# Modulation panels moved from plain fp32 fills to split products inside the feed-forward loops

## The reference

```python
# block 1, layer 0: attention output, one norm per head of 128
o = rms_norm(o, sub_gain) * (1.0 - lam_init);  mix = o.reshape(b, s, 1024) @ w_o
# both layers
h = h + conv_gated_ffn(rms_norm(h, ffn_norm[i]), w_in, conv_w, conv_b, w_out)   # 1024 -> 5632 -> 2816 -> 1024
h = h + (p[i] @ w_proj) * sigmoid(rms_norm(h, ple_norm[i]) @ w_gate)
# block 2, layer i: w_mod[i] is 1024 x 3072; c and c_ctx are single rows
mod_x = silu(c) @ w_mod[i] + b_mod[i];  mod_c = silu(c_ctx) @ w_mod[i] + b_mod[i]
sh, sc, g = split(mod, 3);  hx = rms_norm(x, norm_g[i]) * (1 + sc_x) + sh_x   # and x + g_x * yx at the layer's end
```

## Time and profile before

| | us |
|---|---|
| median of three runs | 1387.62 (1386.74 to 1389.39) |
| the profiled execution | 1387.44 |
| its span in the trace | 1385.7 |
| TensorE busy | 1313.0 |
| VectorE busy | 913.4 |
| ScalarE busy | 683.8 |
| GpSimd busy | 375.7 |

### The profile page before, as it was taken

How to read it: one execution, slowest core, us unless ns; L and a number is a source line. 1 busy time by engine, 2 the same in 40 slices (tenths; PEclk the granted TensorE clock), 3 DMA queues, 4 the chain that set the end, 5 groups by cost and what they waited for, 6 DMA issues and landing times.

```text
span 1385.7 us, 24959 instructions
## 1 busy us (share of the span) xinstructions
PE 1313.0 (95%) x9168; PEld 1146.1 (83%) x9168; DVE 913.4 (66%) x1397; ACT 683.8 (49%) x1207; POOL 375.7 (27%) x390
## 2 busy tenths in 40 slices
PE   6989999999999998999999999999989999999996
PEld 5877899999988886798999999878845588987656
DVE  6868667777767696656777777745257547453674
ACT  5554445555535577634555555434367613422662
...
GB/s 303 176 236 170 185 137 204 183 181 183 182 128 135 131 145 122 1 289 129 214 183 183 183 183 159 88 92 76 102 21 1 22 246 104 182 101 91 46 1 31
DMA packets 52656, 191.60 MB, mean 138 GB/s; under 512 B 6048, under 2 KB 6304, under 8 KB 52320
## 3 DMA queue, kind: packets, MB, share of 16 engines
...
q10 hardware_dynamic: 720, 0.57, 0.1%
...
## 4 chain that ended last, share of the span: by engine, by line
PE 72%; DVE 9%; issue 9%; ACT 7%; POOL 2%; DMA 1%; SPq 0%; DVEq 0%; ACTq 0%; POOLq 0%
PE G L400 12%; PE G L402 12%; PE G L401 12%; PE A L400 6%; PE A L402 6%; PE A L401 6%; PE R L525 3%; PE R L606 3%; DVE WL L1050 2%; ACT WH L1657 2%; PE A L928 1%; PE R L400 1%; PE R L402 1%; PE R L401 1%; DMA RAW<-in_wst 1%
## 5 line engine op out<-in xcount | busy, mean ns | idle before, releaser
L1050 DVE TENSOR_TENSOR WL<-RAW,WH 128x1024 fp32r<-128x1024 f32 x295 | 393.7, 1341 | 304.4 <-ACT WH L1657 303.9
L1657 ACT ACTIVATE WH<-RAW 128x1024 fp32r<-128x1024 f32 x295 | 310.5, 1057 | 433.8 <-PE G L402 310.9
L400 PE MATMUL G<-XH,WH 128*128 128x256 f32 (+1 forms) x1336 | 402.1, 301 | 11.3 <-DVE WL L1050 7.5
L401 PE MATMUL G<-XL,WH 128*128 128x256 f32 (+1 forms) x1336 | 398.2, 298 | 0.0
L402 PE MATMUL G<-XH,WL 128*128 128x256 f32 (+1 forms) x1336 | 398.0, 298 | 0.0
L400 PEld LDWEIGHTS G<-XH,WH 128*128 128x128 f32 x1336 | 256.1, 192 | 22.8 <-issue 11.5
L401 PEld LDWEIGHTS G<-XL,WH 128*128 128x128 f32 x1336 | 256.2, 192 | 7.3
L402 PEld LDWEIGHTS G<-XH,WL 128*128 128x128 f32 x1336 | 256.2, 192 | 7.1
L400 PE MATMUL A<-HH,WH 128*128 128x256 f32 x352 | 99.8, 283 | 0.0
L401 PE MATMUL A<-HL,WH 128*128 128x256 f32 x352 | 99.6, 283 | 0.0
L402 PE MATMUL A<-HH,WL 128*128 128x256 f32 x352 | 99.6, 283 | 0.0
...
## 6 DMA issues: line engine op xcount, KB each, us to landing
RAW<-in_wst SPq DMA_DIRECT2D x295, 512.0 KB, 3.6
...
```

What stands on the lines that cost most here:

```text
L400: mm(out, lh, rh, start=start, stop=False, skip_group_check=True)
L401: mm(out, lh, rl, start=False, stop=False, skip_group_check=True)
L1050: v.tensor_tensor(WL[:, slot, :], RAW[:, raw, :], WH[:, slot, :].bitcast(F32), ALU.subtract).then_inc(w_lo, 1)
L1657: act(WH[:, slot, :], RAW[:, raw, :], ACT.Copy).then_inc(w_hi, 1)
```

## The change

- 16 of the 48 modulation panels stay plain fills, all of them before and behind the attention of layer 0: 12 ahead of it, five in each of its 18 steps instead of six, then 14, 6 and 6. All other fills are gone.
- The other 32 panels are stored in another order (128 rows of two k blocks by 512 columns each) and are done as split products, 16 in each feed-forward. GpSimd's queue loads a panel into one of four slots (gathers), ACT makes its rounded copy RH at the end of a turn (high), GpSimd the rest RL after its hidden work (rest), and TensorE does four matmuls of 32 stationary columns by 512 (refill): after each of tiles 7 to 21, and the sixteenth between the last two down products. The stationary side SCR holds silu(c) rounded in two columns and its rest in two more. RH and RL are single buffers. Four panels give one row of 512 results, which ACT copies to YR (row); the fifth copy comes in ple.
- Behind pp, 16 matmuls with a selecting matrix of 4x2 turn and add the rows (turn_gathered), once a layer; DVE adds the biases later (gathered). The turns inside block 1's layer 1 and block 2 are gone.
- The head norm works on a token-major output OTOK: the value product writes tokens on the partitions, GpSimd squares each head as it comes, DVE sums per head and scales by one number per token and head, and TensorE transposes into the A banks, from which ACT and DVE make XH and XL, in two groups of four heads.
- The embeddings are split into XH and XL 8 and 9 in the feed-forward's opening, so that pp needs no HH and HL, and pp is followed at once by the gathering and pg. The squares of H for pg's norm are made by ACT (squared) and summed by GpSimd (sum_of_parts). The order of XH in layer 0's pg follows GATE.

```diff
+        SCR = sb("SCR", [P, KD, 32], F32R)
...
-        OT0 = B[:, 4096:6144].rearrange("p (n t) -> p n t", t=T)
+        OTOK = B[:, 4096:6144].rearrange("p (a c) -> p a c", a=2)
...
+        YR = B[0:32, 2048:4608]
+        RR = RM[:, 0:4, :]
+        RH = XH[:, 12:16, :].rearrange("p n t -> p (n t)")
+        RL = XL[:, 12:16, :].rearrange("p n t -> p (n t)")
...
+            def refill(layer, s, i):
+
+                if s == 0:
+                    pe.wait_ge(r_y, i + (2 + 5 * layer))
+                pe.wait_ge(r_lo, i * 4 + (5 + PLAIN * layer + s))
+                for c in range(2):
+                    for w in (RH, RL):
+                        m = mm(O[0:32, :], SCR[:, 2 * s + c, :], w[:, 512 * c:512 * c + 512],
+                               start=(s == 0 and c == 0 and w is RH), stop=(s == 3 and c == 1 and w is RL),
+                               skip_group_check=True)
+                m.then_inc(m_used, 1)
+
+            def turn_gathered(layer):
+
+                pe.wait_ge(r_y, 1 + 5 * (layer + 1))
+                for t in range(PLAIN):
+                    m = mm(O[:, 2 * t:2 * t + 2], YR[0:4, 512 + t * P:512 + (t + 1) * P], SEL, start=True, stop=True,
+                           skip_group_check=True)
+                m.then_inc(m_tr, 1)
...
-                for k in range(2):
-                    m = mm(out[:, k * P:T], V0[:, k, h * P:(h + 1) * P], pt[:, 0, k, k * P:T], start=(k == 0),
-                           stop=(k == 1), skip_group_check=True)
+                for qt in range(2):
+                    for k in range(qt + 1):
+                        m = mm(out[:, qt * P:(qt + 1) * P], pt[:, 0, k, qt * P:(qt + 1) * P], V0[:, k, h * P:(h + 1) * P],
+                               start=(k == 0), stop=(k == qt), skip_group_check=True)
...
+            def heads_turn(g):
+
+                for tt in range(2):
+                    pe.wait_ge(hn_ok, 2 * g + tt + 1)
+                    for i in range(4):
+                        m = nc.tensor.transpose(A[2 * g + tt][:, i * P:(i + 1) * P],
+                                                OTOK[:, tt, (4 * g + i) * P:(4 * g + i + 1) * P], IDT)
+                    m.then_inc(hn_tr, 1)
...
             pe.wait_ge(tm_ev, 8)
             pe.wait_ge(tm_v, 4)
+            fill(12)
             pe.wait_ge(bias_ok, 1)
-            attention("l0", scores_l0, value_l0, 6)
-            for c in range(4):
-                fill(5)
-                head_stat(HN["l0_o"] + c, ONES)
-            fill(48)
+            attention("l0", scores_l0, value_l0, 5)
+            fill(14)
+            heads_turn(0)
+            fill(6)
+            heads_turn(1)
+            fill(6)
             for u in range(4):
-                gemm_unit(U0["l0_o"] + u, START["l0_o"] + 2 * u, 0, KD, 8, 2, fresh=XS["l0_o"] if u == 0 else None)
-            turn_modulators(0, A[0])
+                gemm_unit(U0["l0_o"] + u, START["l0_o"] + 2 * u, 0, KD, 8, 2,
+                          fresh=[XS["l0_o"] - 4] * 4 + [XS["l0_o"]] * 4 if u == 0 else None)
+            turn_modulators(A[0])
...
-                                if fresh is not None and k == 6:
-                                    fill(8)
...
                 hidden(0, p0, u0 % 2, u0 // 2, p0, XS[tag])
                 row_stats(tag)
                 hidden(1, p0 + 2, (u0 + 1) % 2, (u0 + 1) // 2, p0 + 2)
-                for d in range(2):
-                    q = p0 + 4 + 3 * d
-                    fill(4)
-                    if layer == 0 and d == 0:
-                        pe.wait_ge(m_ok, 1)
-                    hidden(d, q, (u0 + d) % 2, (u0 + 2 + d) // 2, q)
-                    down(d, q + 2, hb + 1 + d, q + 2, d == 0, False)
-                with pe.Fori(0, 9) as i:
-                    for d in range(2):
-                        q = p0 + 10 + 3 * d
-                        hidden(d, q, (u0 + d) % 2, (u0 + 4 + d) // 2 + i, q + 6 * i)
-                        down(d, q + 2, hb + 3 + d + 2 * i, q + 2 + 6 * i, False, False)
+                def tile(j, i=0, filled=None):
+
+                    q = p0 + 4 + 3 * (j - 2)
+                    hidden(j % 2, q, (u0 + j) % 2, i * 2 + (u0 + j) // 2, i * 12 + q)
+                    down(j % 2, q + 2, i * 4 + (hb + j - 1), i * 12 + (q + 2), j == 2, False)
+                    if filled is not None:
+                        refill(layer, filled, i)
+
+                if layer == 0:
+                    pe.wait_ge(m_ok, 1)
+                for j in range(2, 7):
+                    tile(j)
+                with pe.Fori(0, 3) as i:
+                    for d in range(4):
+                        tile(7 + d, i, d)
+                for d in range(3):
+                    tile(19 + d)
+                    refill(layer, d, 3)
                 down(0, p0 + 64, hb + FT - 1, p0 + 64, False, False)
-                fill(8)
+                refill(layer, 3, 3)
                 down(1, p0 + 65, hb + FT, p0 + 65, False, True)
...
             def ple(layer):
                 a, b = f"pp{layer}", f"pg{layer}"
-                fill(24)
                 pe.wait_ge(p_hi, layer + 1)
                 pe.wait_ge(p_lo, layer + 1)
                 for u in range(4):
-                    gemm_unit(U0[a] + u, START[a] + u // 2, 4 * (u % 2), 2, 0, 2, xh=HH, xl=HL)
-                    if u % 2:
-                        fill(8)
+                    gemm_unit(U0[a] + u, START[a] + u // 2, 4 * (u % 2), 2, 8, 2)
+                turn_gathered(layer)
                 for u in range(4):
-                    gemm_unit(U0[b] + u, START[b] + 2 * u, 0, KD, 8 - 8 * layer, 2, fresh=XS[b] if u == 0 else None)
+                    gemm_unit(U0[b] + u, START[b] + 2 * u, 0, KD, GATE[layer], 2, fresh=XS[b] if u == 0 else None)
                     if u == 0:
                         row_stats(b)
...
-            fill(8)
...
-            fill(HELD * KD - fills[0])
...
-            wide_unit(0, XS["a"], None, lambda: turn_modulators(2, O))
+            wide_unit(0, XS["a"], None, None)
...
-            fill(MODS * KD - fills[0])
...
+            def heads_summed(g):
+
+                dv.wait_ge(hn_sq, 4 * g + 4)
+                v.tensor_reduce(token_sum(g, 8), HRS[:, :, :].rearrange("p a (h d) -> p (a h) d", h=4), AX,
+                                ALU.add).then_inc(hn_ss, 1)
+
+            def heads_applied(g):
+
+                sc = token_scale(g, 8)
+                dv.wait_ge(hn_rt, g + 1)
+                v.reciprocal(sc, sc).then_inc(hn_rc, 1)
+                dv.wait_ge(hn_rc, g + 1)
+                for tt in range(2):
+                    o = OTOK[:, tt, 512 * g:512 * g + 512].rearrange("p (h d) -> p h d", h=4)
+                    v.tensor_tensor(o, o, sc[:, 4 * tt:4 * tt + 4].unsqueeze(2).broadcast_to([P, 4, P]),
+                                    ALU.mult).then_inc(hn_ok, 1)
+
...
+            def heads_rest(g):
+
+                for tt in range(2):
+                    xn[0] += 2
+                    dv.wait_ge(x_hi, xn[0])
+                    t = slice(tt * P, (tt + 1) * P)
+                    v.scalar_tensor_tensor(XL[:, 8 + 4 * g:12 + 4 * g, t], A[2 * g + tt].rearrange("p (k t) -> p k t", k=4), SUBG,
+                                           XH[:, 8 + 4 * g:12 + 4 * g, t].bitcast(F32), ALU.mult,
+                                           ALU.subtract).then_inc(x_lo, 2)
+
+            attention("l0", bias_l0, None, 0, 16)
+            heads_summed(0)
+            attention("l0", bias_l0, None, 16)
+            heads_applied(0)
+            heads_summed(1)
+            heads_applied(1)
+            heads_rest(0)
+            heads_rest(1)
...
             add_out("l0_o", 2, "ffn0", False)
-            modulators(0, A[0], [(0, 0, 4)])
+            modulators()
+            dv.wait_ge(m_sil, 1)
+            link(v.tensor_copy(SCR[:, :, :], SC[:, :, :]))
+            link(v.tensor_tensor(SCR[:, :, 2:4], SC[:, :, 0:2], SCR[:, :, 0:2].bitcast(F32), ALU.subtract))
+            v.memset(SM[:, 34:35], 0.0).then_inc(r_y, 1)
+            v.memset(SM[:, 39:40], 0.0).then_inc(r_lo, 4)
...
+                dv.wait_ge(p_hi, layer + 1)
+                v.tensor_tensor(XL[:, 8:10, :], PIN[:, layer, :, :], XH[:, 8:10, :].bitcast(F32), ALU.subtract).then_inc(p_lo, 1)
+                for j in range(2, 6):
+                    p = p0 + 4 + 3 * (j - 2)
+                    turn(j % 2, (u0 + j) % 2, j, p, p + 3, p + 3, hb + j)
...
                 nxt[0] = p0 + 67
+                ahead(p0 + 65)
...
-                v.tensor_tensor(HL[:, :, :], PIN[:, layer, :, :], HH[:, :, :].bitcast(F32),
-                                ALU.subtract).then_inc(p_lo, 1)
-                x_rest(H, f"ple{layer}", 8 - 8 * layer, KD)
+                x_rest(H, f"ple{layer}", GATE[layer], KD)
...
+            attention("l0", out_l0, 0, 18)
+            heads_root(0)
+            attention("l0", out_l0, 18)
+            heads_out(0)
+            heads_root(1)
+            heads_out(1)
+            rows_out()
...
+                if layer == 0:
```

(89 more changed lines are left out.)

218 lines of the change are left out of this document (87 added, 131 removed).

## The result

The changed kernel takes 1409.6 us (median of 4, 1406.3 to 1410.8) against 1387.2 for the kernel before: ratio 1.0155, 95% interval 1.0134 to 1.0177. Slower, as forecast, by 22.5 us where 14.4 were forecast. Its traced execution took 1406.29 us (span 1404.6), so the trace holds 18.9 us of it. It was the shortest of the four, 3.4 us under their median.

The account below looks back on a forecast made before the run. TensorE, busy 1313 of 1385.7 us, was read as the bound. The terms -5.3 - 11.3 + 0.8 + 25.4 + 10.0 - 9.6 - 5.0 - 3.6 + 13 gave +14.4, so 1402 us; range 1381 to 1420.

Parts of the forecast that it names:

- Attention of layer 0: Layer 0's attention: five fills a unit save 3.9 us, the slow clock after the bias_ok wait 1.4; sum -5.3 us.
- Head norm: Last value product to first l0_o product: 19.9 us becomes 8.6, so -11.3 us, from -9.5 to -12.5.
- Loop: Feed-forward loops: 14 of 16 refills a layer add 12.7 us, twice, +25.4; turns of 9.55 us, no stall.
- Exits: End of last hidden product to end of last down: 10.7 becomes 15.9 us, +5.0 a layer, +10.0 in all.
- Embeddings: Last down product to first pg product: pg begins at 10.3 us, saving 9.6 in layer 0, 5.0 in layer 1.
- Fills in front of waits: Nine places, such as feed-forward openings, ple0, wide_unit 0, b_q: removing the fills only lengthens the waits, nothing saved.
- Later stages: wide_unit 0: early gathering removes the blocked WL, -2.6; other transposes and the fills before context_ahead -1.0.
- The clock: TensorE's clock falls to 0.50 around longer idle times; nine falls at 1.5 us, +13 us, bounds 0 and +20.
- A: Rival: the clock hardly falls, idle times being short or cut by stray products; 1384 to 1391 us; chance 0.20.
- B: Rival: TensorE's work decides and the waits shift away; -21, with the blocked wait 1365 us; chance 0.09.
- C: Rival, loop: GpSimd's subtraction and DVE's two-input work fill the turn; 1415 to 1450 us; chance 0.14 with D.
- D: Rival: a 512-column product with 32 weight columns costs no less than two fills; chance 0.14 together with C.

## Why the prediction was right or wrong

The direction, the places and most of the terms held; the clock's term was mis-sized. By its own steps, against the traced execution:

- Attention of layer 0: -5.3 predicted, -4.5 measured. With the fills' 3.9 taken as predicted, 0.6 is left for the slow clock, not 1.4; in the kernel before, unread products at that wait gave 0.2.
- Head norm: -11.3; -10.9 (9.0 us against 8.6).
- Embedding copy: +0.8; 0.4 at each opening's second wait, +0.8. It stayed with the clock up.
- Loop: +25.4; +25.2, after that 0.4 is taken out of each layer's 13.1. Tiles come 9.55 apart, TensorE unbroken, one subtraction 2.41 (median).
- Exits: +10.0; 2 x 5.3 = +10.6 where the clock is held up by unread products. TensorE idles 5.34, inside the 4 to 6.
- Embeddings: -14.6; -14.2. The two-column products took 3.73 us (predicted 3.7).
- Fills in front of waits: nothing saved, shown by taking them out of the kernel before.
- Later stages: -3.6; -3.4. The blocked WL is gone.
- **The clock: +13 predicted; +15.3 in the trace** (openings 1.5 and 1.5, exits 1.8 and 1.9, pg 1.5 twice, layer 1's attention 2.4, wide_unit 0 1.2, stage a 0.9, b_q 1.2; some of these are what the known terms leave of a stage). This is the term that was mis-sized. For its nine falls at 1.5 us there came eleven new stretches, five of them 6.8 us and longer, and one old one grew. Two of the eleven, at the openings' second waits, cost nothing. The one that I had not listed was the dearest, and came where the idle time did not change at all: 1.91 us in layer 1's attention, at 550.11 before with the clock at 1.00, at 548.26 after with 0.50.

So the trace's +18.9 is +3.6 of all other terms (-4.5 - 10.9 + 0.8 + 25.2 + 10.6 - 14.2 - 3.4) and 15.3 of clock. The median is another 3.6 longer, and that part stays open. I would put it down to the clock too, which would make it some 19, but the record does not bear this out: the other three executions took 1409.0 to 1410.8 us with mean granted clocks of 0.972, 0.969 and 0.973, against 0.970 in the traced one, and the longest has the highest. Only the traced one can be cut into stages. Against the trace the forecast missed 4.5: 2.3 in the clock, 2.2 in small errors of the other terms, nearly all to the same side.

The rivals: A needed a mean clock not below 0.98; it was 0.970. B needed the waits to shift away; the run without the fills refutes it. C did not come, but my margin was wrong. I set it at 1.1 us (8.4 of 9.55 us exclusive) by adding up work; the ring's 9.4 left 0.16. By that ring every tenth of a us over some 2.6 a subtraction would have gone into each turn, as C said, though by another sum than mine. That no stall came in the loop was a near thing, not the 1.1 us of room that the prediction saw. D: the refill's four products took 0.91 us, so it is refuted.

The Trainium skill, "TensorE: Matmul & The Clock Gate", Part 1, says that the low clock is the default and activity lifts it. This case agrees as far as activity goes: 162 products without use took 15.3 us off the median. One stretch in which TensorE was busy all through and the clock stood at 0.50 is in the last section.
